# Recurrent layer: the shared half tile of a head's weights is held as a whole tile with zeros

## The reference, cut to what matters

```
h = x @ w_in
xm, z, gates, q_mem = split(h)                       # xm is 768 wide: 4 heads x 192
xc = silu(conv(xm))                                  # along the tokens, 5 taps
q = einsum('bshd,hde->bshe', heads(xc), w_qkv[0])    # each head has its own 192 x 192 weights
k = einsum('bshd,hde->bshe', heads(xc), w_qkv[1]) * 192 ** -0.5
v = einsum('bshd,hde->bshe', heads(xm), w_qkv[2])
# then, for each head, two chunkwise recurrences (forward and backward) over 8 chunks:
#   num = (q k^T * decay) v + iexp * q C ;  h = num / max(|den|, floor) ;  C = cexp * C + (wexp * k)^T v
```

## Time and profile before

| | us |
|---|---|
| median of the runs shown | 3922.69 |
| the profiled execution, its own time | 3928.44 |
| its span in the trace | 3926.8 |
| TensorE busy (matmul) | 3522.1, 90% of the span |
| VectorE, ScalarE, GpSimd busy | 1927.5, 1375.1, 357.4 |
| mean granted clock of TensorE | 0.903 |
| line 2013, its 256 MATMULs | 193.5 (64.6, 64.5, 32.2 and 32.2 in four shapes) |

### The profile page before, as it was taken

One profiled execution on the slowest core, in us unless ns is written; L12 is line 12 of the kernel. 1 busy time (PEld: TensorE's weight loads), 2 busy tenths in 40 slices (PEclk: granted clock), 3 DMA queues, 4 the chain that ended last, 5 costly groups with the idle time before them and its releaser, 6 DMA issues. The chain is left out here.

```text
span 3926.8 us, 50998 instructions
## 1 busy us (share of the span) xinstructions
PE 3522.1 (90%) x19671; PEld 2704.6 (69%) x19671; DVE 1927.5 (49%) x3394; ACT 1375.1 (35%) x2544; POOL 357.4 (9%) x289
## 2 busy tenths in 40 slices
PE   8999997899979999994969999789978998997899
PEld 6884475798848645554748888578965577896557
DVE  4526545658556413337445655543245444314554
ACT  2016630647540112224216655620144421014442
POOL 0100000323220000000002332300010000001000
PEclk9999988899989756667979999889979999997999
DMA  6525012869764100001245877621100032110003
GB/s 207 165 70 188 22 76 108 311 252 372 280 232 152 50 0 1 1 1 54 81 150 213 336 280 263 261 83 33 32 1 1 1 129 71 33 32 1 1 10 131
DMA packets 250232, 459.85 MB, mean 117 GB/s; under 512 B 44867, under 2 KB 117911, under 8 KB 249625
## 3 DMA queue, kind: packets, MB, share of 16 engines
q1 hardware_dynamic: 231577, 389.70, 28.2%
q0 software_dynamic: 18432, 67.12, 4.5%
HBM read 380.72 MB, written 73.33 MB: 116 GB/s over the span
## 5 line engine op out<-in xcount | busy, mean ns | idle before, releaser
L1727 PE MATMUL psum<-high_in,e_rowsT_high 128*128 128x256 f32 (+1 forms) x1080 | 330.3, 324 | 5.4 <-DVE e_rowsT_low L174 5.4
L1728 PE MATMUL psum<-high_in,e_rowsT_low 128*128 128x256 f32 (+1 forms) x1080 | 326.2, 320 | 0.0
L174 POOL TENSOR_TENSOR low_down<-w_down,high_out 128x1024 fp32r<-128x1024 f32 x64 | 192.6, 3027 | 326.3 <-ACT high_out L1801 326.3
L1727 PEld LDWEIGHTS psum<-high_in,e_rowsT_high 128*128 128x128 f32 x1080 | 206.5, 191 | 22.3 <-issue 6.1
L1728 PEld LDWEIGHTS psum<-high_in,e_rowsT_low 128*128 128x128 f32 x1080 | 207.0, 192 | 16.2
L3428 DVE TENSOR_REDUCE mla_low<-psum 128x1 f32<-128x256 f32 (+7 forms) x128 | 91.0, 752 | 145.7 <-PE psum L3294 145.7
L1856 POOL COPY e_index<-moe_ids 128x1 uint32 (+1 forms) x49 | 9.5, 195 | 1557.8 <-POOLq L84 927.7
L174 DVE TENSOR_TENSOR low_up<-w_up,high_in 128x1024 fp32r<-128x1024 f32 x128 | 148.0, 1218 | 0.0
L174 DVE TENSOR_TENSOR low_gate<-w_gate,high_in 128x1024 fp32r<-128x1024 f32 x128 | 147.9, 1218 | 0.0
L283 PE MATMUL psum<-ring_low,s_x_high 128*128 128x512 f32 (+3 forms) x768 | 136.0, 320 | 4.0 <-DVE ring_low L174 4.0
L279 PE MATMUL psum<-ring_high,s_x_high 128*128 128x512 f32 (+3 forms) x768 | 134.4, 317 | 5.6 <-DVE ring_high L169 5.6
(11 more groups left out here) (591 smaller groups left out, 8064.7 us busy)
## 6 DMA issues: line engine op xcount, KB each, us to landing
w_gate<-in_exp_w_gate SPq DMA_DIRECT2D x32, 2048.0 KB, 10.2
w_up<-in_exp_w_up SPq DMA_DIRECT2D x32, 2048.0 KB, 15.2
w_down<-in_exp_w_down SPq DMA_DIRECT2D x32, 2048.0 KB, 22.0
ada<-in_ada_w SPq DMA_DIRECT2D x24, 1024.0 KB, 7.6
expert_rows<-e_out POOLq DMA_DIRECT2D x47, 512.0 KB, 7.0
expert_rows<-zero_row SPq DMA_DIRECT2D x33, 512.0 KB, 6.9
token_rows<-x SPq DMA_DIRECT2D x32, 512.0 KB, 2.6
x<-token_rows SPq DMA_DIRECT2D x24, 512.0 KB, 6.9
```

The lines of the kernel that those rows point to most:

```text
L174: return eng.tensor_tensor(low, whole, high, ALU.subtract)
L1727: pe.matmul(dst, rows_high[:, k, :], w_high[:, k, cols], start=(k == 0), stop=False)
L1728: pe.matmul(dst, rows_low[:, k, :], w_high[:, k, cols], start=False, stop=False)
```

## The change

A class `HeadWeights` takes the place of the tile `wq`. For each of the three matrices and each head it holds two weight tiles of 128 rows: j = 0 is the tile of the head's whole feature tile, j = 1 the one of the shared feature tile, in which the 64 rows of the neighbour are zero. `pieces_of` now gives (j, feature tile) with the whole tile always first, and every product of lines 2013 and 2173 reads all 128 rows of the feature tile. The tile grows from 3 x 6 x 192 to 3 x 4 x 2 x 192 columns. The load becomes 12 DMAs in place of one (three matrices, two parities of heads, two parts), with the same bytes, and GpSimd writes the zeros in six memsets of 64 rows by 2 x 192. TensorE waits for all 12 loads and all 6 memsets where it waited for the one load. Nothing else changes: the number of products, their columns, and the engines that empty the banks stay.

```diff
 def pieces_of(h):
-    lo, hi = h * ML_DH, (h + 1) * ML_DH
-    return [(f, slice(max(lo, f * P) - f * P, min(hi, (f + 1) * P) - f * P)) for f in range(lo // P, (hi + P - 1) // P)]
+    whole, shared = (3 * h // 2, 3 * h // 2 + 1) if h % 2 == 0 else ((3 * h + 1) // 2, (3 * h - 1) // 2)
+    return [(0, whole), (1, shared)]
+
+class HeadWeights:
+    def __init__(self, core):
+        self.w = core.mem.at("ml_wqkv", AT_WORK, [P, 3, ML_HEADS, 2, ML_DH])
+        self.dram = core.io["ml_w_qkv"][0]
+        self.parts = {0: ((0, slice(0, P), 0), (1, slice(0, P // 2), P)), 1: ((1, slice(P // 2, P), 0), (0, slice(0, P), P // 2))}
+        self.loads = 3 * ML_HEADS * 2 // 2
+
+    def load(self, sp, loaded):
+        for a in (2, 0, 1):
+            for parity in range(2):
+                for j, rows, d0 in self.parts[parity]:
+                    src = self.dram[a, parity::2, d0:d0 + rows.stop - rows.start, :].rearrange("h d e -> d h e")
+                    sp.dma_start(self.w[rows, a, parity::2, j, :], src).then_inc(loaded, 16)
+
+    def clear(self, pool, cleared):
+        for parity, rows in ((0, slice(P // 2, P)), (1, slice(0, P // 2))):
+            for a in range(3):
+                pool.memset(self.w[rows, a, parity::2, 1, :], 0.0).then_inc(cleared, 1)
+
+    def of(self, a, h, j):
+        return self.w[:, a, h, j, :]
...
-                        lambda w, a=a, n=n, half=half: [(wq[rows, a * ML_TILES + f, n * HF:(n + 1) * HF],
-                                                         xcT[rows, f, half * BANK:(half + 1) * BANK]) for f, rows in pieces_of(h)],
+                        lambda w, a=a, n=n, half=half: [(wq.of(a, h, j)[:, n * HF:(n + 1) * HF],
+                                                         xcT[:, f, half * BANK:(half + 1) * BANK]) for j, f in pieces_of(h)],
...
-            jobs.append((lambda w, t=t: [(xcT[rows, f, t * P:(t + 1) * P], wq[rows, ML_TILES + f, :]) for f, rows in pieces_of(h)],
+            jobs.append((lambda w, t=t: [(xcT[:, f, t * P:(t + 1) * P], wq.of(1, h, j)) for j, f in pieces_of(h)],
...
-            sp.dma_start(wq[:, :, :], w_view).then_inc(s["weights_loaded"], 16)
+            wq.load(sp, s["weights_loaded"])
...
-                    for k, (f, rows) in enumerate(pieces_of(h)):
-                        mm = pe.matmul(bank[5 + n % v_banks][:, 0:ML_DH], xmT[rows, f, t * P:(t + 1) * P],
-                                       wq[rows, 2 * ML_TILES + f, :], start=(k == 0), stop=(k == 1))
+                    for j, f in pieces_of(h):
+                        mm = pe.matmul(bank[5 + n % v_banks][:, 0:ML_DH], xmT[:, f, t * P:(t + 1) * P], wq.of(2, h, j),
+                                       start=(j == 0), stop=(j == 1))
...
-            pe.wait_ge(s["weights_loaded"], 16)
+            pe.wait_ge(s["weights_loaded"], 16 * wq.loads)
+            pe.wait_ge(s["weights_cleared"], 6)
...
+        @block.gpsimd
+        def _(pool):
+            wq.clear(pool, s["weights_cleared"])
```

More of the change, by code:

```diff
@@ L1957, in ml_layer @@
     vals = m.at("ml_v", AT_XT, [P, TILES, ML_HEADS, ML_DH + 1])
-    wq = m.at("ml_wqkv", W, [P, 3 * ML_TILES, ML_DH])
+    wq = HeadWeights(core)
     hs = m.at("ml_hs", AT_X, [P, TILES, ML_HEADS, ML_DH])
-    view = core.io["ml_w_qkv"][0].rearrange("a h d e -> (a h d) e").rearrange("(n p) e -> p n e", p=P)
-    table = gates_and_values(nc, core, gatesT, view, wq, xmT, vals)
+    table = gates_and_values(nc, core, gatesT, wq, xmT, vals)
     for h in range(ML_HEADS):
@@ L2113, in __init__, with gates_and_values @@
         self.a, self.E, self.nuT = a, E, nuT
-def gates_and_values(nc, core, gatesT, w_view, wq, xmT, vals):
+def gates_and_values(nc, core, gatesT, wq, xmT, vals):
     m = core.mem
@@ L2157, in gates_and_values @@
     v_banks = 3
-    with stage(nc, "weights_loaded", "values_ready", "values_copied", "loaded", "gates_turned", "steps", "exps", "abs_ready", "log_ready", "summands_ready", "sums_ready", "a_ready", "a_turned",
+    with stage(nc, "weights_loaded", "weights_cleared", "values_ready", "values_copied", "loaded", "gates_turned", "steps", "exps", "abs_ready", "log_ready", "summands_ready", "sums_ready", "a_ready", "a_turned",
                "cummax_ready", "cummax_turned", "diag_ready", "peaks_ready", "exponents_ready", "exps_ready", "neg_ready", "neg_turned") as (block, s):
```

## The result

The changed kernel took 3780.14 us in the median of three runs (3775.88 to 3782.36) against 3922.69: a ratio of 0.9634, 95% interval 0.9612 to 0.9655. That is 142.6 us less, where 160 were forecast (3763 us, range 3750 to 3818). A second measurement on another chip, five rounds beside the kernel before, gave 0.9637 (0.9619 to 0.9655), 3796.67 against 3936.69 us. The profiled execution took 3775.88 us, with a span of 3774.2.

The account below looks back on a forecast made before the run. TensorE was taken to set the pace of values and products, at half clock with gaps at height changes; 34.4 - 1 + 99.6 + 27.2 = 160.2 us off the 3922.7 median gave 3763 us, range 3750 to 3818.

Parts of the forecast that it names:

- The gaps of the changed heights go: Values and q, k, key products: each change of height costs 0.30 us a piece at half clock; with one height it vanishes.
- In the products it is the same: q, k and keys: weight loads wait at each height change as in the values; pieces take 1.95 and 0.94 us.
- The clock rises in all five stages: Values and four heads' products: granted clock goes from 0.50 to 1.00 after 5 us, costing 2.5 us a stage.
- Part 1, values: The values' products: 58.4 us falls to 24.0, which is 34.4 us less.
- Part 2, load: Twelve weight loads in place of one, ahead of the values: 1 us of delay, ends 0 and 11; memsets hidden.
- Part 3, products: q, k and keys of each head: 46.2 us falls to 21.3, 24.9 less a head, 99.6 for four.
- Part 4, the start of the recurrence: Spread and raw scores inherit full clock: 13.6 us falls to 6.8 a head, 27.2 less for four; ends 0 and 27.2.
- Sum: Whole kernel: 34.4 - 1 + 99.6 + 27.2 = 160.2 us less, giving about 3763 us.
- The first rival: Values and products: gaps go but the clock stays at 0.50; 50 us less, 3873 us; chance 0.06.
- The second: q and k: clock rises for 128 weight columns but not for their 96; 106 us less, 3817 us; chance 0.07.

Follow-up runs that it names:

- 64-row run: The kernel before with both pieces of a head cut to the lower 64 rows; one execution took 3885.4 us, the layer 418.4 us.
- repeat: The changed kernel as it is, measured again beside the kernel before on one chip; 3796.67 against 3936.69 us, ratio 0.9637.
- keys at two heights: The changed kernel with the keys alone at 128 and 64 rows by turns again; 3823.89 us, ratio 0.9723.
- early values: The changed kernel, but TensorE waits before the values only for the four loads of their own weights; 3778.02 us, ratio 0.9636.
- all rows: The kernel before with both pieces taking all 128 rows, real neighbour weights instead of zeros, still one load; one execution took 3779.75 us.
- 96 rows: The kernel before with both pieces of a head cut to the lower 96 rows; one execution took 3782.04 us, the layer 313.0 us.
- raw scores first: The changed kernel with TensorE's raw scores (96 rows) moved ahead of the spread (64 rows) in the recurrence; 3773.03 us, ratio 0.958.

## Why the prediction was right

The mechanism held at each step but one size; the sum was 8 us too high in the trace and 18 in the medians.

- *The gaps of the changed heights go.* Right; shown by the 64-row run without any rise of the clock. "In the products it is the same" was not quite so: for q and k, with 96 weight columns, the gap is 0.24 us (1.95 less 2 x 0.853), not 0.30. The sum doesn't use it.
- *The clock rises in all five stages.* Right. The delay was 4.3 us in the values and 5.2 to 5.3 in heads 1 to 3, with 5 assumed; head 0 lost 1.7 us instead of 2.5. Its share is partly luck: behind the same 2.94 us the clock fell in four traces (changed, repeat, keys at two heights, early values) and stayed up in three (all rows, 96 rows, raw scores first).
- *Part 1, values:* 24.0 us forecast, 24.0 measured, though with a shorter delay than assumed.
- *Part 2, load:* 1 us forecast, 1.6 measured. An issue cost 0.64 us, between my two ends of 0.42 and 1.39; the six memsets 2.31 us for 2.0, hidden.
- *Part 3, products:* 21.3 a head forecast, 20.8 and three times 21.7 to 21.8 measured. 98.8 us for four heads instead of 99.6.
- *Part 4, the start of the recurrence* is the term that was mis-sized: 27.2 us forecast, 21.2 measured. Three heads gave 6.0 to 6.3 us instead of 6.8, as the exponentials begin 8.1 us into the stage, not 7.6. My estimate halved 0.213 us a MATMUL to 0.107, and at full clock they take 0.118. The weight loads fill 3.64 of the 3.81 us of the spread there, so they may be what binds; no run tests it. Head 3 gave 2.8, since the clock fell. I had written that 64 rows "didn't raise" the clock and let a fall be an end of the range. The runs show that it doesn't fall from the 64 rows alone, for in heads 0 to 2 they ran at 1.00; it falls more often behind the longer break and, as far as twelve starts show, not with the raw scores first. What decides in the single case stays open. The recurrence behind such a start was 1.3 us slower as well.
- *Sum:* 34.5 - 1.6 + 98.8 + 21.2 - 0.6 is 152.3, against the layer's 152.2 us; the 0.6 are the recurrences, which I had left as they were. The other 10 us to the 142.6 of the medians are the places of the two profiled executions: the one of before lay 5.7 us above its median, the one of after 4.3 us below its own. The repeat shows that such differences arise in a stage far ahead; that none of the 10 us is a cost of the change isn't shown, as said above.

The first rival (gaps alone, 50 us) is what the 64-row run did, 48.6 us. The second (the clock doesn't rise for 96 weight columns) fell: it rose in q and k, 5.2 to 5.3 us behind their start.

## What to carry to other kernels

Two costs of TensorE can hide in one line of a profile that says "busy": read the idle time of the weight loads ("issue") for what each change of height costs, and the granted clock beside it. Where products of different heights alternate, make the height one, by zeros if need be, for the empty rows cost nothing here but the load of the weights in more parts (1.6 us); where that isn't possible, order the pieces so that equal heights meet. And a stage that has reached the high clock hands it on to the next only over a short break: behind 3.3 us of idle time every head's products began at half clock, behind 2.9 us the clock fell in four traces of seven, and behind 1.1 us in 5 starts of 23. Shorten or fill the break where you can, and put the taller products first behind it.

## What the runs showed of the hardware

- A change between 128 and 64 rows cost 0.30 us with 128 weight columns and 0.24 us with 96 at half clock, and 0.20 us with 128 at full clock (the keys: 8.3 - 5.4 us over 15).
- Two pieces of 64 rows in different halves ran side by side (kernel before, border of heads 0 and 1: four weight loads in 0.51 us).
- Products 64 rows high, dense, ran at 1.00 for the 3.8 us of the spread in heads 0 to 2 of the changed kernel, but didn't bring the clock up from 0.50 in 43 us; products 96 rows high did, in 5.5 us in the values.
- Each of twelve DMAs of 96 and 192 KB, in rows of 768 bytes, cost SyncE 0.64 us to issue and landed 2.8 us later.
- Between executions of one program the granted clock of a stage can differ: where TensorE is busy for some 80% of the time it was 0.89 in one and 0.70 in the other, which moved the time by 11 us (repeat against first trace of the changed kernel).
